# Two transformer blocks on one core: a lagged second half at the end of block one, and the two attentions of block two in the other order

## The reference

```python
# first block, end
merged = sigmoid(ga) * (ya @ w_branch_a) + sigmoid(gb) * (yb @ w_branch_b)
mix_out = merged @ w_out
ple = sigmoid(x @ w_ple_gate) * (p @ w_ple)
x = layer_norm(DEEPNORM_ALPHA * x + mix_out + ple, ln_g, ln_b)

# second block
h = rms_norm_2(x, g_mix_norm) * (1.0 + scale_m) + shift_m
proj = h @ w_in      # q_lat, kv_lat, k_rope, fq, fk, fv, f_logit, gate_a, gate_b
q  = rms_norm_2(q_lat, g_q_lat) @ w_q_up      # 8 heads, 64 plain + 32 rotated columns
kv = rms_norm_2(kv_lat, g_kv_lat) @ w_kv_up
o_mla = causal_attention(q, k, v)                            # the latent attention
o_fox = causal_attention(fq, fk, fv, cumsum(log_sigmoid(f_logit + b_forget)))   # the gated one
x = x + gate_m * ((sigmoid(gate_a) * (o_mla @ w_o_mla)
                   + sigmoid(gate_b) * (o_fox @ w_o_fox)) @ w_out)
# then a router and 64 experts of width 256, six per token, plus a shared expert
```

## Time and profile before

| | us |
|---|---|
| median of 3 runs (lowest, highest) | 1148.98 (1148.11, 1151.58) |
| the profiled execution's own time | 1146.6 |
| its span, first to last instruction | 1144.9 |
| PE busy | 1062.0 (93%) |
| DVE / ACT / POOL busy | 550.1 / 390.1 / 335.6 |
| mean granted TensorE clock | 0.958 of full |

### The profile page before, as it was taken

The page is one execution under the profiler, slowest core; times in us unless marked ns, Lnnn a source line. Parts: engine busy times, 40 slices in busy tenths (PEclk is TensorE's granted clock), DMA queues, the critical chain, the costliest instruction groups (busy, mean ns, idle before and its releaser), DMA issues. The chain is left out here.

```text
span 1144.9 us, 12825 instructions
## 1 busy us (share of the span) xinstructions
PE 1062.0 (93%) x4990; PEld 705.6 (62%) x4990; DVE 550.1 (48%) x987; ACT 390.1 (34%) x668; POOL 335.6 (29%) x261
## 2 busy tenths in 40 slices
PE   6999999989999696999987999999999999999993
PEld 4887888768877565887776635353544444444442
DVE  5978677758765766655644312222222122222214
ACT  4645675546433424657333211121111111111212
POOL 1058946594683057274400000000000000000000
PEclk9999999989998797999996999999999999999997
DMA  9656653956675264455349389999999999999991
GB/s 327 207 184 221 221 202 111 338 178 252 199 275 186 74 194 147 128 172 204 112 185 376 120 343 416 412 417 418 417 418 417 417 416 417 416 417 417 418 374 38
DMA packets 93933, 320.65 MB, mean 280 GB/s; under 512 B 6288, under 2 KB 7328, under 8 KB 76976
## 3 DMA queue, kind: packets, MB, share of 16 engines
q1 hardware_dynamic: 92832, 316.07, 72.3%
q0 software_dynamic: 752, 3.22, 0.8%
q10 hardware_dynamic: 288, 0.52, 0.1%
HBM read 318.74 MB, written 1.05 MB: 279 GB/s over the span
## 5 line engine op out<-in xcount | busy, mean ns | idle before, releaser
L757 PE MATMUL ps<-hl,L 128*128 128x512 f32 (+1 forms) x1216 | 389.0, 402 | 11.8 <-DVE rlo L1501 8.5
L757 PEld LDWEIGHTS ps<-hl,L 128*128 128x128 f32 x1216 | 232.5, 194 | 60.9 <-issue 14.6
L1501 DVE TENSOR_TENSOR rlo<-ring,hl 128x1024 fp32r<-128x1024 f32 (+1 forms) x154 | 209.0, 1376 | 119.5 <-ACT hl L1164 118.7
L757 PE MATMUL ps<-rlo,L 128*128 128x512 f32 (+1 forms) x608 | 241.1, 397 | 0.0
L757 PE MATMUL ps<-slots_all,xe 128*64 128x512 f32 (+1 forms) x1056 | 226.9, 582 | 0.8 <-DVE rt L2236 0.8
L1164 ACT ACTIVATE hl<-ring 128x1024 fp32r<-128x1024 f32 (+1 forms) x154 | 159.9, 1057 | 196.6 <-PE ps L757 79.3
L718 POOL TENSOR_SCALAR ring<-ring,st 128x512 f32<-128x512 f32 x84 | 168.8, 2009 | 0.0
L746 POOL CAST two<-ident 64x128 fp32r<-64x128 f32 x64 | 19.1, 298 | 501.1 <-PE ps L757 499.6
L757 PEld LDWEIGHTS ps<-slots_all,xe 128*64 128x64 f32 x1056 | 73.9, 137 | 131.7 <-issue 128.5
L757 PEld LDWEIGHTS ps<-rlo,L 128*128 128x128 f32 x608 | 117.3, 193 | 25.0
L720 POOL TENSOR_TENSOR macc<-macc,ring 128x512 f32<-128x512 f32 x84 | 119.4, 1421 | 7.0
(11 more groups left out here) (208 smaller groups left out, 902.2 us busy)
## 6 DMA issues: line engine op xcount, KB each, us to landing
slots_all<-in_w_exp_gate SPq DMA_DIRECT2D x64, 1024.0 KB, 20.0
slots_all<-in_w_exp_up SPq DMA_DIRECT2D x64, 1024.0 KB, 15.9
slots_all<-in_w_exp_down SPq DMA_DIRECT2D x64, 1024.0 KB, 16.7
ring<-in_w_in SPq DMA_DIRECT2D x49, 1024.0 KB, 5.4
ring<-in_w_mod SPq DMA_DIRECT2D x24, 1024.0 KB, 7.3
ring<-in_w_out SPq DMA_DIRECT2D x8, 1024.0 KB, 5.1
ring<-in_w_ple_gate SPq DMA_DIRECT2D x4, 1024.0 KB, 5.2
ring<-in_w_branch_a SPq DMA_DIRECT2D x4, 1024.0 KB, 6.1
```

The costliest lines, as they stand in the source:

```text
L757: return e.matmul(o, l, r, start=start, stop=stop)
L1501: return e.tensor_tensor(o, a, b, op)
```

## The change

It has two parts.

**A run with a lag.** `bb0 bb1`, `wo0 wo1` and `c0` become runs in which the half m = 1 comes four pieces behind the half m = 0 (table `BEHIND`). A run of eight pieces has 12 steps: four with only m = 0 (six matmuls), four with both (m = 0 of piece s and m = 1 of piece s - 4), four with only m = 1. `mT` and `hT` are turned half by half: `mT` of m = 0 after step 9 of the `bb` run, of m = 1 after step 1 of the `wo` run, `hT` of m = 0 between the `wo` run and `c0`, of m = 1 after step 2 of `c0`. A piece's buffers come free when both halves have used it, so ACT and DVE can prepare less far ahead. The evacuations, the layer norm and the RMS norm are written out by halves on DVE and ACT. The layer norm takes its mean from sums that come with the evacuation and its variance from a square on ACT. `hT` is no transposition any more: the row scale goes into a diagonal matrix (`DIAG`, 128 columns) and PE multiplies x by it, a float32 matmul.

**The second block.** After `c0` come `fq`, `fk`, `lT`, the cumulative gates, the first half of `fv`; then the up-projections and `qf`/`kf` (`middle`), the second half of `fv`, and the gated attention's steps between `fv` and `g2`. The rotation of the latent queries and keys (`rope_lat`) is spread over `g0` and `g1`, `qm`/`km` are turned after `g1`, and the latent attention's steps lie in `g2` to `of1`. `of` comes before `om`. In the string of names the `m` loads move too: in front of `of0` now stands `m10`, between `om0` and `om1` stands `m11`.

```diff
-                     "pg0 pg1 ple ba0 ba1 m8 bb0 bb1 m9 wo0 wo1 ln c0 fq up fk m4 fv g0 m5 g1 g2 m10 g3 om0 om1 "
-                     "of0 m11 of1 wp0 wp1").split():
+                     "pg0 pg1 ple ba0 ba1 m8 bb0 bb1 m9 wo0 wo1 ln c0 fq fk up fv g0 m4 g1 m5 g2 g3 m10 of0 of1 "
+                     "om0 m11 om1 wp0 wp1").split():
...
+        BEHIND = (("bb0 bb1", 4), ("wo0 wo1", 4), ("c0", 4),)
...
+                for s in range(len(ps) + lag):
+                    t = sum(len(v) for v in steps_of.values())
+                    halves = [(ps[s], 0)] if s < len(ps) else []
+                    halves += [(ps[s - lag], 1)] if s >= lag else []
...
-            while at_piece < min(g + NH, npieces) and all(
-                    freed_by(q) <= g for q in range(pieces[at_piece][0] - NS + 1)):
+            while at_piece < npieces and (at_piece < NH or used[at_piece - NH] < t) and all(
+                    freed_by(q) <= t for q in range(pieces[at_piece][0] - NS + 1)):
...
-        MLA_IN = {"fv": (0, 1), "g0": (2, 3), "g1": (4, 5)}
-        FOX_IN = {"g2": (0, 1), "g3": (2, 3), "om0": (4,), "om1": (5,)}
+        PAIRS_IN = {"fv": ((), ((0, 0),)), "g0": (((0, 1),), ((0, 2),)), "g1": (((0, 3),), ((0, 4),)),
+                    "g2": (((0, 5), (4, 0)), ((4, 1),)), "g3": (((4, 2),), ((4, 3),)), "of0": (((4, 4),),), "of1": (((4, 5),),)}
...
+            project("bb0", L0, l_ready("ybT"), {9: lambda: merged_turn(0)})
+            project("wo0", L1, l_ready("mT"), {1: lambda: merged_turn(1)})
+            h_turn(0)
+            project("c0", L0, h_ready, {2: lambda: h_turn(1)})
...
+            project("bb0", at={3: lambda: bb(0, 0), 7: after_bb1, 10: lambda: completed("mT", tokens=(0,))})
+            bb(1, 1)
...
+            def wo(c, m):
+                o = R[:, m, half(c)]
+                done(f"wo{c}", m)
+                wait_mine()
+                e.scalar_tensor_tensor(out=o, in0=PS[bank_of[f"wo{c}"] + m][:, :], scalar=1.0, in1=o, op0=ALU.mult,
+                                       op1=ALU.add, accum_out=st[:, 160 + 2 * m + c:161 + 2 * m + c]).then_inc(ev_v.sem, 1)
...
+            def first_rows():
+                wo(1, 0)
+                less_mean(0)
+                variance(0)
+                wo(0, 1)
+                scale(0)
+                scaled(0, 0)
+                scaled(0, 1)
+
+            def second_rows():
+                w.wait_ge(sq_a, 2)
+                mean_square(0, rt_v)
+                wo(1, 1)
+                diagonal(0)
+                less_mean(1)
+                variance(1)
+                h_shift(0)
+                scale(1)
+                scaled(1, 0)
+                h_low(0, 0)
+                h_shift(4)
+                scaled(1, 1)
+                h_low(0, 4)
+
+            project("wo0", at={2: lambda: completed("mT", tokens=(1,)), 3: lambda: wo(0, 0), 7: first_rows, 9: second_rows})
...
+            project("fv", L0, h_ready, {1: middle})
```

More of the change, by code:

```diff
@@ L386, in two_blocks @@
         MOD_IN, MOD_SUM = {}, {}
+        SUM_AT = {}
         for c in mods:
@@ new lines, in _ @@
+            turn("km", lambda m, j: KM[:, m, 96 * j:96 * j + 96], lambda m, j0: w.wait_ge(roped2, 4), width=96)
+            project("g2", L0, h_ready)
+            turn("ofT", lambda m, j: mla_o[:, m, 128 * j:128 * j + 128], lambda m, j0: wait_read(("o2", 3)), (0,))
+            project("g3", L0, h_ready)
+            for name in ("of0", "of1"):
+                project(name, L1[:, :, 4:8, :], l_ready("ofT"))
+            turn("omT", lambda m, j: mla_o[:, m, 128 * j:128 * j + 128], lambda m, j0: wait_read(("o2", 7)), (0,))
@@ L1368, in _, with first_squares, roots @@
                 act(pair_of("hT", m, j0, 0), tmp, ACT.Copy).then_inc(th.sem, 1)
+            def first_rows():
+                rounded("mT", tokens=(1,))
+                act(st[:, 255:256], ones[:, 0:1], ACT.Sqrt)
+            def first_squares():
+                square(0, 0)
+                square(0, 1)
+            def roots():
+                square_root(0)
+                ln_square(1)
+            project("wo0", at={2: first_rows, 7: lambda: ln_square(0), 8: first_squares, 9: roots})
+            h_round(0, 0)
+            square(1, 0)
+            h_round(0, 4)
+            square(1, 1)
+            square_root(1)
+            h_round(1, 0)
+            h_round(1, 4)
             project("c0", lambda m: PR[:, m, :])
@@ L1970, in _ @@
                 w.wait_ge(*evacuated("c0", m))
+                x = tt(FZ[:, 8 * m:8 * m + 8], PR[:, m, 416:424], brd[:, 448:456], ALU.add)
+            x.then_inc(fz_v, 1)
+            for m in range(2):
                 mine(e.bn_stats(st[:, 160 + 12 * m:166 + 12 * m], PR[:, m, 0:256]))
@@ L2036, in rope_lat @@
                      .then_inc(roped2, 1)
-            job = side.add(rope_lat())
-            project("fk", fox_evac("fk", FK))
-            side.finish(job)
-            for m in range(2):
-                x = tt(FZ[:, 8 * m:8 * m + 8], PR[:, m, 416:424], brd[:, 448:456], ALU.add)
-            x.then_inc(fz_v, 1)
+            project("fq", fox_evac("fq", FQ))
             w.wait_ge(fz_a, 1)
```

531 lines of the change are left out of this document (289 added, 242 removed).

## The result

| | before | after |
|---|---|---|
| median (lowest, highest; runs) | 1150.28 (1148.11, 1152.72; 4) | 1136.04 (1134.93, 1138.23; 4) |
| profiled execution, its own time | 1146.6 | 1138.23 |
| its span | 1144.9 | 1136.5 |
| mean granted TensorE clock | 0.958 | 0.963 |

A forecast was written before the change was run, and what follows sets the result against it. The experts' PE work was taken as fixed, so dense-part savings reach the end one for one. Stretch one 8.5 plus stretch two 6.6 gave 15.1 us; from the median 1149.0 that is 1133.9, stated as 1134, range 1122 to 1147.

The forecast's parts named there:

- What bounds it: PE work on the experts, 438.7 us, stays untouched; what the dense part saves or loses reaches the end one for one.
- Stretch one: Start of `bb0` to end of `c0`: 74.5 us against 83.0, a gain of 8.5, with 9.6 of waits and 1.5 lower clock.
- The wait before wo0: After the `bb` run and modulation sum, PE waits 0.9 us while DVE prepares two pieces, then completes `mT`; clock expected to stay.
- the interface that I weighed: SBUF interface GpSimd shares with VectorE: remainder steps 1.57 us beside POOL against 1.22; at worst 2.7 us, giving 1136.7.
- Stretch two: End of `c0` to end of `wp1`: 14.7 gained, less 4.6 net waits, 2.5 lower clock, 1 small waits: 6.6 us.
- The three waits (11.1): PE's idle before `lT` (2.2), `qm` (2.3) and `km` (6.6) falls away, with 3.6 us of lower clock.
- The late load of `om1`: It needs the slot of `m10`'s second half: waits of 2.1 and 3.3 us, net 4.6 more, plus 2.5 lower clock.
- the rotation has `g0` and `g1` (22 us and three attention steps): In the second block, the rotation's cover, instead of today's window of 11.5 us.
- 2 us to spare: Margin given to the load of `g2`, which hangs on `m4`; small waits elsewhere were put at 1 us.
- (a): Rival: the late load is covered and the clock holds in stretch one; gain 25 us, 1124 us; chance 0.15.
- (b): Rival: at the first block's end the clock never comes back between small waits; 7 us slower, 1156 us; chance 0.08.
- (c): Rival: the ring starves, with pieces and loads each 1 us late (12), eating the gain; 1146 to 1151 us; chance 0.07.

The follow-up runs named there:

- x4: Changed kernel with the first tokens' half of `mT` rounded (ACT) and completed (DVE) two pieces of weights earlier; ratio to before 0.9878.
- x6: Changed kernel with PE's sum of `m4` one block earlier, at `g2` for `g3`, nothing else moved; 1130.08 us, ratio to before 0.9829.
- x5: Changed kernel with DVE's latent rotation begun in `fv` and spread thinly behind the pairs of `g0` and `g1`, none with the pieces; ratio to before 0.9874.
- x12: Changed kernel with `m4`'s sum at `g2`, the rotation spread thinly, and the middle pair of `g0` and `g1` one piece earlier; 1126.71 us, ratio 0.9813.
- x9: Changed kernel with `m4`'s loads moved behind `c0`'s and `m5`'s in front of `g1`'s, their sums at `fv` and `g3`; 1136.27 us, ratio 0.9898.
- x11: Changed kernel with the load of `m9`, and with it its sum, moved behind `c0`; 1140.01 us, ratio to before 0.9931.

## Why the prediction was right, and where it was not

**What bounds it.** Right. The experts' stretch is 438.8 us for 438.7, and the dense part's gain reached the end but for 0.5.

**Stretch one.** 74.4 us measured, 74.5 forecast, but that is luck: two errors of some 2.7 us cancel. The waits came to 6.9 and not 9.6: 0.18 (0.3 forecast), 2.23 (0.9), 0 (0.2), 2.50 (3.4), 0.36 (1.4), 0 (0.5), 0.59 (2.1), 1.01 (0.8). PE's work came to 67.5 and not 64.9. The diagonal product is about as I took it from the upper bound: 2.05 us for a group's 8 products at the full level (a row counts each of them twice, as x16), where 8 transpositions take half of 1.91 in the earlier trace rows. Over both halves that is +2.2 for the 1.9. What was mis-sized is the clock: over 61.1 + 2.2 the 67.5 leaves 4.2 us of lower level, for which I had 1.5. I had argued from one row, the 2.18 us before `qu`, that waits near 2 us leave the clock alone. Behind 2.23 and 2.50 the windows show 0.66 and 0.67.

**The wait before wo0.** 2.23 for 0.9. I had two pieces ahead of `mT`. The order list of the change has three, and so has DVE's row, and they took 1.67 each beside POOL, not 1.22:

```profile
341.52 5.00 DVE L1602 TENSOR_TENSOR rlo<-ring,hl 128x1024 fp32r<-128x1024 f32 x3
```

The slower steps are the interface that I weighed and left out of the sum. Here the two together cost 1.3 us of wait, and with the lower clock behind it 3. But x4, which takes the wait away, gains nothing in the stage, so it was no term of its own. In this the model of the sum was wrong: it added up waits that trade against each other.

**Stretch two.** 1.8 us gained for 6.6. The three waits (11.1) and their clock (3.6) did fall away: there is no wait from `fq` through the latents, and stage B begins without one. The late load of `om1` was found and sized well: 2.23 before the weighting (2.1 forecast), 2.81 before `omT` (3.3), with ACT at 540.4 waiting for it, and 2.5 of lower clock by x6 (2.5 forecast). x6 also shows the chain that I had written down, from `m4`'s sum to `m10` to the slot. The step that failed is the sentence "the rotation has `g0` and `g1` (22 us and three attention steps)". It counts the time that is there, and not the order in which DVE gets to it. The rotation's steps stand with the pieces, ahead of the pair's maxima, and the pair needs those within the block. PE lost 4.8 us of wait and 5.1 of lower clock there, nearly 10 us, and my condition "no wait over 1 us between `fq` and `g2`" was broken at this place. How much of the 10 is the rotation's own stays open: x5, which takes it out of the way, gets back 2.8 in B, since ACT's table loads and the load of `g2` stand right behind it. For that load I had allowed "2 us to spare" and put 1 us for all small waits, and in x5 it cost 2.42 of wait at pair (0,3). On the other side, the small waits of the attention steps and before `om` and `of` came to 2.7 us for 5.3 before.

**The rivals.** (a) asked for the late load to be covered and the clock to hold in stretch one, at 1124. x6 covers the load and gives 1130. The clock of stretch one was down in it as in after, and the rotation was in the way. x12 comes nearest, at 1126.71. (b) has its mechanism in the windows, short waits with 1.2 GHz behind them, but at four places and for a few us each; the point at which it decides, 17 us of work at the lower level beyond before, was not reached, since the mean clock rose from 0.958 to 0.963. (c) did not occur: PE waits for no `rlo` or `hl` inside a run in after. Experiments with other orders have such a wait once each (0.59 us in x4, 0.8 to 1.0 in x9 to x11).

**The signs.** The wait before `mT` (0.18), the end of `c0` (74.4 us), the wait before `omT` with ACT behind its load, and the experts' stretch came as written. The wait before the first h product was 2.50 for 3 to 4, `wp1` ended at 594.65 for 588, and the window behind `wo0`'s start was at 0.66, though not for all of `wo`.

**The range and the forecast.** 1136.04 lies 2 us above 1134 and inside 1122 to 1147, on the side of "faster". By the terms it was less good than that: of 15.1 us the stages of the two profiles show 10.4, and the ratio says 12.3. In part the nearness is luck, in stretch one by terms that cancel, in the median by the scatter of four runs.

## What to carry to other kernels

When work is moved under cover, check the order on the engine that does it: a side job that rides on another loop is in front of whatever that loop's next consumer needs, and 22 us of cover are worth nothing if its steps stand ahead of the one result that PE waits for. Where engines pass work round in a chain, size the chain and not the waits: two edits here each took away 2 us of wait at one place and the stage kept its length. And look at who frees a buffer before looking at who fills it: the largest gain here (6.2 us in the stages) was to let a sum run one block earlier, because an accumulator held POOL, POOL held a ring slot, and the slot held a weight load.
